# One expert loop that alternates 64-row and 128-row visits in place of two loops with a barrier between them

## The reference

```
act = silu(h @ w_gate[e]) * (h @ w_up[e])
out = out + combine[:, e:e + 1] * (act @ w_down[e])
```

## Time and profile before

| | us |
|---|---|
| median of the 3 runs | 3375.32 |
| lowest and highest run | 3372.16, 3378.34 |
| the profiled execution's own time | 3381.49 |
| its span in the trace | 3379.8 |
| TensorE busy (matmuls), share of the span | 2632.9, 78% |
| DMA, mean over the span | 220 GB/s |

### The profile page before, as it was taken

The page is one execution under the profiler, slowest core; times in us unless marked ns, Lnnn a source line. Parts: engine busy times, 40 slices in busy tenths (PEclk is TensorE's granted clock), DMA queues, the critical chain, the costliest instruction groups (busy, mean ns, idle before and its releaser), DMA issues. The chain is left out here.

```text
span 3379.8 us, 34102 instructions
## 1 busy us (share of the span) xinstructions
PE 2632.9 (78%) x11124; PEld 1356.0 (40%) x11124; DVE 871.4 (26%) x1534; ACT 415.0 (12%) x779; POOL 279.9 (8%) x415
## 2 busy tenths in 40 slices
PE   6996779768985998867775999649699837777692
PEld 4431144234433553524432444225376424433240
DVE  1221253000004795410000000160357520000004
ACT  1011140000001001000000000010055100000000
POOL 3001140200001000020000000000000010000001
PEclk8998878898997998879997999869899959999796
DMA  9426611779954112279997899442001149999783
GB/s 345 135 78 222 210 13 57 292 315 343 335 218 142 50 50 77 75 279 421 423 423 305 323 333 338 166 137 75 0 13 36 33 177 418 423 423 422 273 296 118
DMA packets 150429, 744.57 MB, mean 220 GB/s; under 512 B 13552, under 2 KB 15264, under 8 KB 101168
## 3 DMA queue, kind: packets, MB, share of 16 engines
q1 hardware_dynamic: 100784, 592.46, 45.3%
q0 software_dynamic: 35568, 115.04, 9.9%
q10 hardware_dynamic: 13968, 35.66, 2.8%
HBM read 664.24 MB, written 79.46 MB: 220 GB/s over the span
## 5 line engine op out<-in xcount | busy, mean ns | idle before, releaser
L681 PE MATMUL ps<-w_ring,arena 128*64 128x256 f32 x3136 | 369.1, 390 | 133.3 <-DMA w_ring<-in_e_up 59.7
L604 PE MATMUL ps<-w_ring,arena 128*128 128x512 f32 x960 | 429.4, 602 | 7.2 <-ACT arena L600 7.2
L232 PE MATMUL ps<-x_feat,w_ring 128*128 128x512 f32 (+1 forms) x1152 | 421.5, 528 | 7.9 <-ACTq L145 3.7
L681 PEld LDWEIGHTS ps<-w_ring,arena 128*64 128x64 f32 x3136 | 221.5, 140 | 285.2 <-DMA w_ring<-in_e_gate 91.8
L232 PEld LDWEIGHTS ps<-x_feat,w_ring 128*128 128x128 f32 x1152 | 220.6, 192 | 208.0 <-issue 192.9
L604 PEld LDWEIGHTS ps<-w_ring,arena 128*128 128x128 f32 x960 | 183.3, 194 | 227.0 <-issue 222.5
L706 PE MATMUL ps<-w_ring,arena 128*64 128x512 f32 x784 | 182.3, 607 | 41.0 <-DMA w_ring<-in_e_down 35.4
L626 PE MATMUL ps<-w_ring,arena 128*128 128x512 f32 x480 | 211.3, 593 | 2.3 <-ACT arena L621 2.3
L324 PE MATMUL ps<-w_ring,x_feat 128*128 128x512 f32 x448 | 198.4, 606 | 13.7 <-ACTq L145 12.1
L955 PE MATMUL ps<-w_ring,fcol 128*2 128x512 f32 x384 | 182.0, 630 | 3.2 <-issue 2.3
L690 DVE TENSOR_TENSOR arena<-arena,ps 128x256 f32<-128x256 f32 x49 | 20.7, 421 | 629.9 <-PE ps L681 629.9
(11 more groups left out here) (272 smaller groups left out, 2326.9 us busy)
## 6 DMA issues: line engine op xcount, KB each, us to landing
w_ring<-in_e_gate SPq DMA_DIRECT2D x63, 2048.0 KB, 17.5
w_ring<-in_e_up SPq DMA_DIRECT2D x63, 2048.0 KB, 17.9
w_ring<-in_e_down SPq DMA_DIRECT2D x63, 2048.0 KB, 17.2
w_ring<-in_ada_w SPq DMA_DIRECT2D x24, 2048.0 KB, 10.2
w_ring<-in_w_gate SPq DMA_DIRECT2D x16, 2048.0 KB, 10.7
w_ring<-in_w_up SPq DMA_DIRECT2D x16, 2048.0 KB, 10.4
w_ring<-in_w_down SPq DMA_DIRECT2D x16, 2048.0 KB, 8.6
arena<-expert_rows ACTq DMA_DIRECT2D x39, 512.0 KB, 8.6
```

Of the source, the lines that this page charges most:

```text
L232: mm = nc.tensor.matmul(pair(j)[:, t0:t1], w[:, k, c0:c0 + P], x_feat[:, k, t0:t1], start=k == 0, stop=k == KT - 1)
L604: mm = nc.tensor.matmul(bank(2 + part), blk_feat[:, s, k, :], chunk_view(slot, FF)[:, k, :], start=k == 0, stop=k == KT - 1)
L681: mm = nc.tensor.matmul(bank(2 + part)[self.H * c:self.H * (c + 1), 0:256], blk_feat[:, s, i, self.H * h:self.H * (h + 1)], w[:, h, i, 256 ...
```

## The change

The two calls of each engine's expert loop and the `stage()` between them become one call. The loop has `turns = max(doubles, singles) // 4` passes (4, 8 and 8) of four pairs, and a pair is one visit of a single followed by one visit of a double. The ring stays at four slots, and a pair has six chunks in it, empty or not:

```
-        self.chunks = 3 * (self.doubles + self.singles) + 4
+        self.turns = max(self.doubles, self.singles) // 4
+        self.chunks = 24 * self.turns + 4
```

SP loads gate and up of the first single and of the first double before it waits for the scatter (two chunks before, four now), and then goes through the pairs:

```
+            for n, kind in enumerate(kinds):
+                for k, (part, w) in enumerate((("gate", gate), ("up", up))):
+                    c = base + 2 * n + k
...
+            sp.wait_ge(*count(f"{name}.scattered", 32 * m.T))
+            with sp.Fori(0, m.turns) as turn:
+                for b in range(4):
+                    i = turn * 4 + (b + 1)
+                    for n, kind in enumerate(kinds):
+                        c = base + 4 + 6 * b + 3 * n
+                        with sp.If(i < n_used[n]):
+                            for k, (part, w) in enumerate((("gate", gate), ("up", up))):
+                                source = matrix(kind, w, i, part)
+                                sp.wait_ge(w_free, turn * 24 + (c + k - RING + 1))
...
+                        with sp.Else():
+                            for k in range(2):
+                                sp.wait_ge(w_free, turn * 24 + (c + k - RING + 1))
+                                sp.sem_inc(w_landed[(c + k) % RING], 16)
```

TensorE's loop, in which n is 0 for the single and 1 for the double; the waits on `other` keep the shared PSUM banks apart:

```
+            with pe.Fori(0, m.turns) as turn:
+                for b in range(4):
+                    s = (b + 1) % 2
+                    i = turn * 4 + (b + 1)
+                    for n in range(2):
+                        other = 1 - n
+                        c = base + 4 + 6 * b + 3 * n
+                        with pe.If(i < n_used[n]):
+                            pe.wait_ge(*count(at(n, "feat"), i + 1))
+                            pe.wait_ge(*count(at(other, "silu"), i + n))
+                            gate_or_up(n, s, 0, c, turn)
+                            turn_hidden(n, 1 - s, i)
+                            pe.wait_ge(*count(at(other, "hid"), i + n))
+                            gate_or_up(n, s, 1, c + 1, turn)
+                            pe.wait_ge(*count(at(other, "feat"), i + 1 + n))
+                            turn_rows(n, 1 - s, turn * 32 + 16 * ((b + 2) // 2 + 1))
+                            down(n, 1 - s, i, c + 2, turn)
                         with pe.Else():
+                            pe.drain().then_inc(w_free, 2)
+                            pe.sem_inc(summed[at(n, "turned")], 1)
+                            with pe.If(i < n_used[n] + 1):
+                                turn_hidden(n, 1 - s, i)
+                                down(n, 1 - s, i, c + 2, turn)
+                            with pe.Else():
+                                pe.sem_inc(w_free, 1)
```

```
-            moe_blocks_pe(pe, "moe1", Singles(MOE1), chunks)
-            stage(pe, "pe", "singles1")
-            moe_blocks_pe(pe, "moe1", Doubles(MOE1), chunks)
+            moe_blocks_pe(pe, "moe1", MOE1, chunks)
```

More of the change, by code:

```diff
@@ L398, in moe_sems @@
                 shared(name, route_counts(m))
-                for kind, n in (("single", m.singles), ("double", m.doubles)):
-                    shared(f"{name}.{kind}", visit_counts(n))
+                for kind in ("double", "single"):
+                    for part, total in visit_counts(4 * m.turns).items():
+                        shared(name, {f"{kind}.{part}": total})
                     new_sems(f"{name}.{kind}", "stored")
@@ L736, in moe_sp, with matrix @@
-            if kind.kind == "single":
-                sp.wait_ge(*count(f"{name}.scattered", 32 * scatter_tiles[name]))
-            with sp.Fori(0, kind.n // 4) as turn:
+            sp.wait_ge(*count(f"{name}.table", 1))
+            kinds = (Singles(m), Doubles(m))
+            n_used = [kind.used(sp) for kind in kinds]
+            def matrix(kind, w, visit, part):
+                e = sp.value_load(expert_of[0:1, bass.ds(visit + kind.table_at, 1)], min_val=0, max_val=m.E - 1)
+                return kind.weights(w, e, part)
@@ L740, in moe_sp @@
                     i = turn * 4 + (b + 1)
[L741 to L756, removed]
@@ L794, in moe_blocks_pe @@
                     i = turn * 4 + (b + 1)
[L795 to L803, removed]
@@ L815, in moe_blocks_act @@
-        def moe_blocks_act(act, name, kind, chunks):
-            base = chunks.n
[L817 to L835, removed]
-            load_rows(0, 0)
-            load_rows(1, 1)
-            take_features(0, 0)
-            load_rows(2, 0)
-            act.wait_ge(w_free, base + 1)
-            silu(0)
-            take_features(1, 1)
-            load_rows(3, 1)
-            with act.Fori(0, kind.n // 4) as turn:
+                    for n in range(2):
[11 more added lines that the diff above has]
+                            down(n, 1 - s, i, c + 2, turn)
+                        with pe.Else():
+                            pe.drain().then_inc(w_free, 2)
[5 more added lines that the diff above has]
+                                pe.sem_inc(w_free, 1)
+                                pe.sem_inc(summed[at(n, "hid_turned")], 1)
@@ new lines, in moe_blocks_act, with moe_blocks_dve, at, hidden @@
+            for n in range(2):
+                for s in range(2):
+                    act.wait_ge(*count(at(n, f"rows{s}"), 16 * (2 * m.turns + 2)))
+            chunks.n += m.chunks
+        def moe_blocks_dve(dve, name, m, chunks):
+            base = chunks.n
+            kinds = (Singles(m), Doubles(m))
+            def at(n, part):
+                return f"{name}.{kinds[n].kind}.{part}"
+            def hidden(n, s, i):
+                dve.wait_ge(*count(at(n, "silu"), i + 1))
+                kinds[n].hidden(s).then_inc(summed[at(n, "hid")], 1)
+            def outputs(n, s, i, value):
+                dve.wait_ge(w_free, value)
+                dve.wait_ge(*count(at(n, "out_free"), i))
+                kinds[n].take_outputs(s).then_inc(summed[at(n, "y_copied")], 1)
+            n_used = [kind.used(dve) for kind in kinds]
+            for n in range(2):
+                dve.sem_inc(summed[at(n, "y_copied")], 1)
+                dve.wait_ge(w_free, base + 2 * n + 2)
+                hidden(n, 0, 0)
+            with dve.Fori(0, m.turns) as turn:
```

308 lines of the change are left out of this document (155 added, 153 removed).

## The result

The changed kernel takes 3583.46 us (median of 4 runs, 3573.40 to 3587.83) against 3374.41 before (4 runs): a ratio of 1.0614, 95% interval 1.0589 to 1.0639. The forecast was slower, 3412, in a range of 3362 to 3468. The side was right; the size was out by 171 us. The profiled execution took 3573.40 us (span 3571.6) and was the lowest of its runs, where that of before (3381.49, span 3379.8) lay above all four; so the two spans differ by 191.8, the medians by 209.1, and stages are compared by the spans. Some executions are slow (4269.71 us once of the kernel in experiment 3, where the others took 3347 to 3351), and all times given here are of the fast ones.

What follows compares the result with a forecast made beforehand. Singles were taken as DMA-bound, doubles as TensorE-bound. Mixtures came to +2.5, -35.0 and +69.3 us, together +36.8 on the median 3375.3, giving 3412 us; 8-in-10 range 3362 to 3468.

Steps and rivals of the forecast that it cites:

- Pairs: Loop while both kinds are left: single plus double take 34.1 us instead of 38.1, DMA hidden only just; 23 full pairs.
- Rival 1: In the pairs, DMA sets the pace: 36.4 us per pair, 53 us more, 3465 us in all; chance 0.14.
- Start: Each mixture, from first row load to the loop: 33.8 us, of which 6 taken for the row wait.
- the step that named the scatter sharing DMA with two more loads: At each mixture's start, four weight loads precede the scatter wait instead of two; row wait taken as 6 us, bounds 0 and 9.
- Leftovers: Visits after one kind runs out: 23.4 us per single against 16.1, 33.4 per double against 22.0.
- the slow gate: First matmuls of a leftover visit, after idle, run at reduced clock: 6.7 us for a single's gate, warm 3.7.
- the ring argument: Leftover gate load: absent partner's three empty chunks make it wait for the previous visit's down, 8.4 us idle.
- Rival 2: Gap before a leftover's gate: clock stays full, single 21.2 us, double 29.7; 53 us less, 3359 us; chance 0.14.
- rival 3: Leftover visits: clock stays low in up too, 68 us more, 3480 us, or 3636 if all at half; chance 0.06.
- rival 4: Leftover visits: the change does not serialise them, loads are issued early after all, 3240 us; chance 0.03.
- Empty visits: End of each mixture: 12, 24 and 18 empty visits at 1.13 us each, giving ends of 16.3, 29.8 and 23.1 us.

Runs made afterwards that it cites:

- experiment 3: Loops cut to the passes that hold visits, dropping nearly all empty visits: in the changed kernel 3424.22 us, in the kernel before 3350.84 us.
- Experiment 4: Changed kernel with two pairs per pass, and remaining singles of mixtures 2 and 3 in a loop of their own: 3328.21 us, ratio 0.9876.
- experiment 1: Changed kernel with two pairs per pass instead of four: 3449.67 us; kernel before with eight visits per pass instead of four: 3432.03 us.

## Why the prediction was right or wrong

**Pairs: right.** Forecast 34.1 us, measured 34.08, with no wait for weights and DMA at 412 GB/s. Rival 1 (DMA sets the pace) is out. What was left over are the gaps of 0.4 to 1.5 us once per pass. They are gone with two pairs per pass, so they go with the long body.

**Start: right in time, short in place.** From the row load to the loop 34.6 us (643.07 to 677.63; 34.2 and 34.3 in mixtures 2 and 3) against 33.8. But the step that named the scatter sharing DMA with two more loads priced it only behind the row load. It costs before it: 9.7 us in mixture 3, most of the 12.5 outside the stages.

**Leftovers: right in mechanism and nearly in size.** Forecast 23.4 us per single and 33.4 per double, measured 23.9 and 32.8. The wait is 8.4 to 10.1 us where I had 8.4, the slow gate 5.0 to 6.6 where I had 6.7; with two pairs per pass the distance is 23.2. Experiment 4 shows the ring argument: without the partner's chunk numbers the same visits take 16.1. Rival 2 (cheap leftovers), rival 3 (clock stays low: the up behind each gate takes 3.67 us) and rival 4 are out, and so are the leftovers as the cause of the miss.

The granted clock of the leftover stretch is a mean of 0.79, between the two levels of 1.2 and 2.4 GHz: after some 9 us of idle the gate runs slow (0.56 over the 6.51 us of the first) and the rest of the visit at 1.00. The Trainium skill, page "TensorE: Matmul & The Clock Gate", Part 1, has idle TensorE fall to the lower level; the leftovers agree (0.79), and the gaps of 1.6 us in the earlier trace rows did not bring it about.

**Empty visits: the step that failed.** The prediction said "1.13 us each and 0.8 besides. Now 6, 12 and 9 pairs, 12, 24 and 18 empty visits, close the mixtures: with 2.0 to the store 16.3, 29.8 and 23.1 us." The count was right. The price came from a loop whose body was four doubles, and I carried it to one of four pairs, more than twice as long, as though an empty visit's price lay in its branches and drains. The 1.13 us was measured only where no code was fetched, so its range of 0.9 to 1.3 was a range for the wrong mechanism. Measured: 3.0 to 3.6 us each, one code packet after the other at 3.0 us, which is 118.7 of the 142.5 us by which the stages missed. With the fetches gone (two pairs per pass) the stages are 374.7, 658.9 and 630.8 us, against my 369.8, 650.8 and 628.7, so the other terms hold to 15 us in all, of which 7.4 lie in the ends; and 3449.67 lies in my range. Even there the slope was too low: from 12 to 24 empty visits the end grows by 18.2 us, 1.5 each. Four pairs against two differ by 127.4 us in the stages, 111.3 in the ends and 16.1 inside the loops, where matmuls hide most of the fetches.

The Trainium skill, page "Runtime: NRT & Kernel Launch", section "Instruction fetch mechanics", says that each engine keeps little code (128 KiB for PE, 2048 instructions), refilled in blocks of 16 KiB, and that a taken branch to a target outside the current two pages has to fetch it before it goes on. The packets of 16.4 KB agree. An estimate by that page: 71 packets in 8 passes are 8.9 per pass, or 146 KB, just over its 128 KiB for four pairs; scaled by the counts of matmuls and weight loads, eight doubles come to 127 KB and eight singles to 165 KB, on the two sides where experiment 1 found them. The packets of that experiment give less for eight singles, 34 in the four passes of mixture 3, or 139 KB per pass, still above it; the estimate does not explain the 2 packets of the second pass in mixture 2. The same page says that the memory is only two such blocks; the loops of two pairs, 73 KB by this scaling, run with 4 packets in a whole mixture, which does not fit a memory of two blocks; here the measurement decides.

**What stays open.** Whether the limit lies at those 128 KiB or elsewhere between 1280 and 1472 matmuls and weight loads was not narrowed down, nor why eight singles were fetched again in mixture 3 and hardly in mixture 2. A ring of more slots, or chunk numbers that the absent partner does not use up, would also lift the leftovers' wait; neither was tried. The sources of the last 24 us beyond the forecast inside the stages (16 of them tied to the body's length, as above, of which some 10 in the leftovers of mixture 3: 0.7 us each) were not separated further.

## What to carry to other kernels

Before a loop body with runtime branches is made longer, count its instructions on the engine that has most of them, and look at the instruction queue's packets in the profile: an empty or short pass costs what it fetches, here 3 us per 16 KB, not what it executes. When two kinds of work are interleaved over a ring, look at what the ring does once one kind runs out; let the rest run in a loop without its partner. Pairing a DMA-bound visit with a TensorE-bound one is worth its 4 us per pair only where few visits are left without a partner, or where these run by themselves: in mixture 2, with 20 against 14, it gained 34 us. In mixture 3, with 23 against 6, it lost 71 even with the short body, and gained 40 once the leftovers had their own loop.

## What the runs showed of the hardware

Code fetches show only on q8 and in an idle PE sequencer: 216 packets where the short body has 53 cost 134 us while the queue's share of DMA stayed at 0.4%. One packet of 16.4 KB takes 3.0 us when nothing else is left to do, and in full pairs of 34 us the same fetches leave a gap of 0.4 to 1.5 us per pass of four. A stretch with no work on TensorE at all was the critical one, and it was TensorE's. In the end of mixture 3 the granted clock read 0.53 (window above): no matmul ran, so it cost nothing there.
